# Two-block transformer on one core: expert 31's rows joined to the tokens by diagonal products on TensorE, and one root for two norms

## The reference, cut to what matters

```
y = ypad.reshape(-1, D)[dest] * weights[order][:, None]
f = zeros.at[tok].add(y)              # two weighted expert rows for each token
x = x + g2 * f                        # g2: a row of modulation gates
...
h = modulate(rmsnorm(x, norm_mix_g[1]), sh1, sc1)       # layer 1 begins, behind expert layer 0
...
x = rmsnorm(x, final_g)                                 # behind expert layer 1
h = rms_norm(x, attn_pre_norm)                          # layer 2 begins
```

## Time and profile before

| What | Value |
| --- | --- |
| median of three runs | 2109.87 us |
| profiled execution, its own time | 2111.29 us |
| its span, first to last instruction | 2109.4 us |
| PE busy, matmuls | 1954.9 us, 93% of the span |
| DVE, ACT, POOL busy | 653.6, 370.9, 321.7 us |
| moved by DMA | 586.23 MB, 278 GB/s in the mean |
| mean granted TensorE clock | 0.992 of 2.4 GHz |

### The profile page before, as it was taken

One profiled execution on the slowest core, in us unless ns is written; L12 is line 12 of the kernel. 1 busy time (PEld: TensorE's weight loads), 2 busy tenths in 40 slices (PEclk: granted clock), 3 DMA queues, 4 the chain that ended last, 5 costly groups with the idle time before them and its releaser, 6 DMA issues.

```text
span 2109.4 us, 34164 instructions
## 1 busy us (share of the span) xinstructions
PE 1954.9 (93%) x14831; PEld 1224.5 (58%) x14831; DVE 653.6 (31%) x1520; ACT 370.9 (18%) x821; POOL 321.7 (15%) x264
## 2 busy tenths in 40 slices
PE   5999999999999979999999888888789989989998
PEld 4566475555555546546565444444367677675884
DVE  1235273322222234114331111111146031037752
ACT  3133230000000002113320000000021130042131
POOL 0125402000001000114310000000120060040120
PEclk9999999999999999999999999999999999999999
DMA  9585199999999988317299999999984323427221
GB/s 362 124 274 205 56 357 381 427 426 427 426 427 422 426 347 261 118 52 281 95 381 426 427 427 426 427 426 426 407 293 151 131 81 135 145 81 200 81 92 60
DMA packets 133744, 586.23 MB, mean 278 GB/s; under 512 B 19162, under 2 KB 34474, under 8 KB 108880
## 3 DMA queue, kind: packets, MB, share of 16 engines
q1 hardware_dynamic: 117024, 558.65, 67.4%
q10 hardware_dynamic: 10448, 18.88, 3.0%
q0 software_dynamic: 6112, 6.39, 0.9%
HBM read 572.23 MB, written 25.29 MB: 283 GB/s over the span
## 4 chain that ended last, share of the span: by engine, by line
PE 69%; DMA 20%; DVE 3%; issue 3%; ACT 2%; POOL 2%; SPq 1%; DVEq 0%; POOLq 0%; ACTq 0%
DMA RG<-in_moe_w 19%; PE banks L1574 13%; PE banks L2627 8%; PE banks L1599 6%; PE banks L1550 4%; PE banks L2219 4%; PE banks L2629 4%; PE banks L1119 4%; PE banks L683 3%; PE banks L2221 3%; PE banks L2828 3%; PE banks L3039 2%; POOL AR L931 2%; PE banks L341 2%; PE banks L824 2%
## 5 line engine op out<-in xcount | busy, mean ns | idle before, releaser
L1574 PE MATMUL banks<-RG,HT 128*64 128x256 f32 x3616 | 427.8, 390 | 36.6 <-DMA RG<-in_moe_w 33.6
L1574 PEld LDWEIGHTS banks<-RG,HT 128*64 128x64 f32 x3616 | 252.6, 135 | 223.3 <-DMA RG<-in_moe_w 55.5
L1844 POOL DMA_INDIRECT y_rows<-AR x64 | 63.9, 999 | 839.8 <-DVE AR L1613 812.1
L1583 DVE TENSOR_TENSOR AR<-AR,banks 128x256 f32<-128x256 f32 x64 | 38.6, 603 | 479.6 <-ACT AR L1579 428.4
L1599 PE MATMUL banks<-RG,AR 128*64 128x512 f32 x752 | 171.7, 598 | 3.8 <-DVE AR L1592 3.1
L2627 PE MATMUL banks<-HT,RG 128*128 128x256 f32 x768 | 168.0, 380 | 0.8 <-ACT HT L550 0.8
L2627 PEld LDWEIGHTS banks<-HT,RG 128*128 128x128 f32 x768 | 145.4, 190 | 22.8 <-issue 2.4
L1579 ACT ACTIVATE AR<-banks 128x256 f32<-128x256 f32 x64 | 24.5, 383 | 744.6 <-PE banks L1574 744.6
L1550 PE MATMUL banks<-AR 128*128 128x256 bf16 (+1 forms) x1152 | 149.4, 277 | 2.0 <-DVE AR L1538 1.5
L1550 PEld LDWEIGHTS banks<-AR 128*128 128x128 bf16 x1152 | 108.3, 99 | 33.8 <-issue 18.3
L1599 PEld LDWEIGHTS banks<-RG,AR 128*64 128x64 f32 x752 | 50.0, 136 | 94.4 <-issue 83.4
(11 more groups left out here) (490 smaller groups left out, 2392.6 us busy)
## 6 DMA issues: line engine op xcount, KB each, us to landing
RG<-in_moe_w SPq DMA_DIRECT2D x160, 2048.0 KB
AR<-in_moe_w SPq DMA_DIRECT2D x32, 2048.0 KB, 21.5
RG<-in_ada_w SPq DMA_DIRECT2D x24, 2048.0 KB
RG<-in_attn_w_in SPq DMA_DIRECT2D x20, 2048.0 KB
RG<-in_odd_w_in SPq DMA_DIRECT2D x6, 2048.0 KB
RG<-in_ssm_w_in SPq DMA_DIRECT2D x4, 2048.0 KB
AR<-y_rows SPq DMA_DIRECT2D x12, 512.0 KB, 6.1
RG<-in_even_w_in SPq DMA_DIRECT2D x2, 2048.0 KB
```

The source lines that it names most:

```text
L1574: m = pe.matmul(p[64 * h:64 * h + 64, 256 * i:256 * i + 256], x[:, k, :], w[:, h, k], start=k == 0, stop=k == 7, skip_group_check=True)
L1844: g.indirect_dma_start(y, off, E.Y[b], None, bounds_check=2047, oob_is_err=False).then_inc(*event)
```

## The change

In both expert layers the join of tiles 0 and 1 moves from DVE to PE. PE starts the sum in banks 0 to 3 with a product of the identity and the residual rows (pe_own_rows, between expert 31's turns and its down products), adds the one-hot products of expert 31, whose rows DVE now scales by their weight in the slot (dve_y_last), and adds the products of the z rows with diagonals of the weights (pe_joined_rows). The weight for each slot comes from three bf16 parts of WL and eight (four) small products in the table of group 7; the parts and the diagonals are made at expert 12. pe_overflow now stands ahead of the joining products. Squares are read from PSUM, half a row at a time; the first norm's squares are added from two sums. Behind layer 0 the idle products are 10 and not 36. Behind layer 1 AG is not scaled: the turns are products with a diagonal of the norms' common factor. That factor comes from one root of mean(AF^2) + 1e-6 * (mean(x^2) + 1e-6); the root for the output's norm follows behind the turns. The idle products are 30 and don't wait, and of each tile's two banks DVE copies the second to HT. Tiles 2 and 3 of layer 0 stay as they are, but for the weight.

```diff
+                self.W3, self.WS = new(nt, 3, dt=BF), new(1)
...
+            if g == 7:
+                for h in range(2):
+                    for t in range(E.nt):
+                        m = pe.matmul(bank[64 * h:64 * h + 64, 16:19], E.one_hot(7, t)[:, 192:256], E.W3[:, t],
+                                      start=t == 0, stop=t == E.nt - 1, skip_group_check=True)
...
+            if g == 7:
+                vstep(v, v.tensor_reduce(E.WS, bank[:, 16:19], AX, ADD))
...
+        def dve_y_last(v, E, b, event):
+            v.scalar_tensor_tensor(out=E.YL, in0=PS[6 + b], scalar=E.WS, in1=(GATE0[0], GATE1)[E.l], op0=MUL,
+                                   op1=MUL).then_inc(*event)
...
+        def act_joined_squares(act, l, t, junk, name):
+
+            act.wait_ge(*at("last_out", l, t))
+            act.activation(junk[:, 512:1024], PS[2 * t + 1], ACT.Square,
+                           accum_out=ST[:, 8 + t:9 + t]).then_inc(*ev("squares_half", "joined", l, t))
+            act.wait_ge(*at("joined_half", l, t))
+            act.activation(junk[:, 0:512], PS[2 * t], ACT.Square, accum_out=ST[:, t:t + 1]).then_inc(*ev("squares", name))
+
+        def dve_joined_halves(v, l, t, first, second):
+
+            v.wait_ge(*at("last_out", l, t))
+            first(PS[2 * t]).then_inc(*ev("joined_half", l, t))
+            v.wait_ge(*at("squares_half", "joined", l, t))
+            return second(PS[2 * t + 1])
+
+        def pe_own_rows(pe):
+            for t in range(2):
+                for h in range(2):
+                    pe.matmul(PS[2 * t + h], IDN[:], XS[:, t, 512 * h:512 * h + 512], start=True, stop=False,
+                              skip_group_check=True)
+
+        def pe_joined_rows(pe, E, t):
             if t == 0:
                 pe.wait_ge(*at("last_hot", E.l))
                 pe.wait_ge(*at("y_out", E.l, 31))
             for h in range(2):
                 r = slice(64 * h, 64 * h + 64)
-                m = pe.matmul(PS[last_banks(E, t)[h]], E.LP[r, 128 * t:128 * t + 128], E.YL[r, :], start=True, stop=True)
+                pe.matmul(PS[2 * t + h], E.LP[r, 128 * t:128 * t + 128], E.YL[r, :], start=False, stop=False,
+                          skip_group_check=True)
+            pe.wait_ge(*at(f"z_load{t}", E.l, 1))
+            for c in range(2):
+                for h in range(2):
+                    m = pe.matmul(PS[2 * t + h], E.DW[t][c], E.Z[t][c][:, 512 * h:512 * h + 512], start=False, stop=c == 1,
+                                  skip_group_check=True)
+            m.then_inc(*ev("last_out", E.l, t))
...
-                ins = v.scalar_tensor_tensor(out=x, in0=PS[last_banks(E, t)[h]], scalar=E.WL[:, t:t + 1], in1=x, op0=MUL,
-                                             op1=ADD)
+                ins = v.tensor_tensor(x, PS[last_banks(t)[h]], x, ADD)
...
+                if e == 31:
+                    pe_own_rows(pe)
                 pe.wait_ge(*at("h_out", l, e))
                 pe.wait_ge(*landed(("w2", l, e)))
...
+        def dve_last_weights(v, E):
+
+            vstep(v, v.tensor_copy(E.W3[:, :, 0], E.WL))
+            for i in range(2):
+                vstep(v, v.tensor_tensor(E.WL, E.WL, E.W3[:, :, i], SUB))
+                vstep(v, v.tensor_copy(E.W3[:, :, i + 1], E.WL))
+            for t in range(2):
+                for c in range(2):
+                    ins = v.tensor_scalar(E.DW[t][c], IDN[:], E.WT[:, t, c:c + 1], None, MUL)
+            vstep(v, ins)
...
+                if e == 12:
+                    dve_last_weights(v, E)
...
         def pe_odd_begin(pe):
             pe_odd_cols(pe)
-            pe_keep(pe, 36, 3)
+            for t in range(2):
+                pe_joined_rows(pe, E0, t)
+            pe_keep(pe, 10, 5)
             for t in range(2):
                 pe_odd_turn(pe, t)
...
             for i in range(2):
-                v.wait_ge(*at("last_added", 0, i))
-                dve_odd_join(v, i, ev("joined_rows", i))
-            for i in range(2):
+                x = XS[:, i, :]
+                dve_joined_halves(v, 0, i, lambda p: v.tensor_copy(x[:, 0:512], p),
+                                  lambda p: v.tensor_copy(x[:, 512:1024], p)).then_inc(*ev("joined_rows", i))
+                v.wait_ge(*at("squares", ("mix1", i)))
+                vstep(v, v.tensor_tensor(ST[:, i:i + 1], ST[:, i:i + 1], ST[:, 8 + i:9 + i], ADD))
                 dve_rstd(v, ("mix1", i), D, at_=i)
                 dve_diagonal(v, i)
             for i in range(2):
...
             pe_experts(pe, E1, nothing)
+            pe_overflow(pe, E1)
             for t in range(2):
-                pe_last(pe, E1, t)
-            pe_overflow(pe, E1)
+                pe_joined_rows(pe, E1, t)
...
         def act_final(act):
             act.activation(ST[:, 63:64], IDN[:, 0:1], ACT.Sqrt)
             for t in range(2):
-                act.wait_ge(*at("combined", t))
-                act.activation(ar((0, 2)[t] * KK, D), XS[:, t, :], ACT.Square,
-                               accum_out=ST[:, t:t + 1]).then_inc(*ev("squares", ("final", t)))
+                act_joined_squares(act, 1, t, ar((0, 2)[t] * KK, D), ("final", t))
                 act.wait_ge(*at("gained", t))
                 act.activation(E1.Z[t][1], AF[t], ACT.Square,
                                accum_out=ST[:, 2 + t:3 + t]).then_inc(*ev("squares", ("dil", t)))
+            act_root(act, ("dil", 1), n=2, at_=2)
             act_root(act, ("final", 1), n=2, at_=0)
-            act_root(act, ("dil", 1), n=2, at_=2)
-            act.wait_ge(*at("gained", 2))
-            act.wait_ge(*at("dil_scale"))
-            act.activation(W1[1], AG, ACT.Copy, scale=ST[:, 53:54]).then_inc(*ev("dil_scaled"))
             for t in range(2):
-                act_turn(act, "dil", t)
+                act_turn_half(act, "dil", t, 0)
 
         def dve_final(v):
             v.wait_ge(*at("final_loads", 1))
             for t in range(2):
-                v.wait_ge(*at("last_added", 1, t))
-                v.wait_ge(*at(f"z_load{t}", 1, 1))
-                dve_join(v, E1, t, ev("combined", t))
-                v.wait_ge(*at("combined", t))
-                v.tensor_tensor(AF[t], XS[:, t, :], FG, MUL).then_inc(*ev("gained", t))
-            v.wait_ge(*at("gained", 1))
-            v.tensor_tensor(AG, AF[1], PG1, MUL).then_inc(*ev("gained", 2))
-            first, second, s2, w = ST[:, 16:18], ST[:, 18:20], ST[:, 2:4], ST[:, 52:54]
-            dve_rstd(v, ("final", 1), D, n=2)
-            vstep(v, v.tensor_tensor(w, first, first, MUL))
+                dve_joined_halves(v, 1, t, lambda p: v.tensor_tensor(AF[t][:, 0:512], p, FG[:, 0:512], MUL),
+                                  lambda p: v.tensor_tensor(AF[t][:, 512:1024], p, FG[:, 512:1024], MUL)).then_inc(
+                    *ev("gained", t))
+                v.wait_ge(*at("gained", t))
+                v.tensor_tensor(AG[t], AF[t], PG1, MUL)
+            s1, s2, w, a = ST[:, 0:2], ST[:, 2:4], ST[:, 18:20], ST[:, 52:54]
+            v.wait_ge(*at("squares", ("final", 1)))
+            vstep(v, v.tensor_tensor(s1, s1, ST[:, 8:10], ADD))
+            dve_mean(v, ("final", 1), s1, D)
+            v.wait_ge(*at("mean", ("final", 1)))
+            vstep(v, v.tensor_scalar(a, s1, 1e-6, None, MUL))
             v.wait_ge(*at("squares", ("dil", 1)))
-            vstep(v, v.tensor_tensor(s2, s2, w, MUL))
-            dve_rstd(v, ("dil", 1), D, n=2, at_=2, summed=True)
-            v.tensor_tensor(w, first, second, MUL).then_inc(*ev("dil_scale"))
-            v.wait_ge(*at("dil_scale"))
-            v.scalar_tensor_tensor(out=W1[0], in0=AF[0], scalar=w[:, 0:1], in1=PG1, op0=MUL, op1=MUL).then_inc(
-                *ev("normed", "dil", 0))
+            v.scalar_tensor_tensor(out=s2, in0=s2, scalar=1.0 / D, in1=a, op0=MUL, op1=ADD).then_inc(*ev("mean", ("dil", 1)))
+            dve_rstd_pair(v, ("dil", 1), 2, 2)
+            for t in range(2):
+                v.tensor_scalar(DG2[t], IDN[:], w[:, t:t + 1], None, MUL).then_inc(*ev("diagonal", "dil", t))
+            for t in range(2):
+                v.wait_ge(*at("turned", "dil", t, 1))
+                v.tensor_copy(HT[:, 4:8, 128 * t:128 * t + 128],
+                              PS[5 + 2 * t].rearrange("p (k t) -> p k t", k=4)).then_inc(*ev("turned_dve", "dil", t, 1))
+            dve_rstd_pair(v, ("final", 1), 0, 2)
             for t in range(2):
                 v.tensor_scalar(XS[:, t, :], AF[t], ST[:, 16 + t:17 + t], None, MUL).then_inc(*ev("finished", t))
 
         def pe_final(pe):
-            pe.wait_ge(*at("gained", 0))
-            pe_keep(pe, 34, 0)
+            pe_keep(pe, 30, 7)
             for t in range(2):
-                pe_turn(pe, "dil", t, W1[t], (("normed", "dil", 0), ("dil_scaled",))[t], None)
+                pe.wait_ge(*at("diagonal", "dil", t))
+                for b in range(2):
+                    for k in range(4):
+                        m = pe.matmul(PS[4 + 2 * t + b][:, 128 * k:128 * k + 128],
```

(53 more changed lines are left out.)

22 lines of the change are left out of this document (9 added, 13 removed).

## The result

The changed kernel took 2120.63 us (median of 5 runs, 2119.0 to 2121.85) against 2109.87 for the kernel before (5 runs beside it): ratio 1.0052, 95% interval 1.0041 to 1.0063. That is slower by 10.8 us, beyond the 0.2% that a measurement can tell, and above the range forecast. The profiled execution took 2119.6 us, its span is 2117.8 (2109.4 before): 8.4 us more. The other 2.4 us of the 10.8 are those by which the two profiled executions lie off their kernels' medians. The shares of the chain hardly changed.

A forecast was written before the change was run, and what follows sets the result against it. The prediction took the PE queue, and chains on which PE waits, as the bound. Its terms, -1.8 + 0.2 + 3.3 = +1.7 us on 2109.9, gave 2111.6 us, with a range of 2107 to 2117.

The forecast's parts named there:

- part 2: Branch over the overflow experts, ahead of joining products: PE back at 779.0 and 1542.9; 0.6 us lost in second layer.
- PE works without gaps behind the stretches: Behind both layers' stretches from down products to projection, PE has no gaps, so a shift there shifts the end.
- Part 1: Four own-row products between expert 31's turns and down products, both layers: 3.43 us, down products 2.9 us later.
- rival (a): Branch exposed, reached only after the down products; PE 5.4 us later in second layer, half clock 2.2; 2122.8, chance 0.16.
- Part 3: Joining on PE in both layers: 4.3 us per tile, 8.6 for both; DVE's joins and last additions removed.
- Part 4: First layer behind the join: DVE back only at 784.9, projection at 796.7 against 798.5, so -1.8 us.
- Part 5: Second layer behind the join: idle products end 1.7 us after diagonals; projection 1563.0 against 1559.6, +3.3 us.
- Part 6: Expert loops: eight small products added to group 7's table, +0.2 us in first layer; transfers hide the second layer's four.
- The sum: Whole kernel: -1.8 + 0.2 + 3.3 = +1.7 us on the median, giving 2111.6 us.

The follow-up runs named there:

- the second layer alone: Join on PE and the one root in the second layer only, first layer as in the kernel before: 2116.36 us, ratio 1.0046 against the kernel before.
- the one with 128 more: Changed kernel plus 32 idle products (128 PE instructions) in experts 20 to 27 of the second layer: 2118.91 us, ratio 1.0038 against the kernel before.
- own rows spread: Changed kernel, own rows spread over PE's waits, 18 idle products for 30: 2110.06 us; with the second layer as before the change: 2109.49 us.
- own rows behind: Changed kernel with the four own-row products behind expert 31's down products in both layers: 2115.01 us, ratio 1.0035 against the kernel before.

## Why the prediction was wrong

The step that failed most is the price of the branch in the second layer (part 2): 0.6 us of idle PE and no clock drop stood there, and the runs showed 2.5 us and 1.7 us of half clock. The second is the sentence that PE works without gaps behind the stretches: the rest grew by 2.7 us. The parts one by one:

- **Part 1, own rows:** right. They take 3.44 us, and the down products start 2.9 us later in both layers.
- **Part 2, the branch:** the mechanism was right (reached while the queue still works), its size too small. The load of the count was reached with the first down product (772.7 and 1536.1), 2.9 us behind the end of the wait, in the later half of the 1.5 to 3.5 us. In the first layer PE was back 13.7 us behind the up products, as forecast, since the branch was the short one there. The second layer's branch took 6.1 us, as assumed, but 1542.9 is what the early end of the range gives with it. The late end, 1544.7, is what came: 1543.11 with up products that start 1.6 us earlier. PE lost 2.5 us ahead of the joined rows where 0.6 stood: **+1.9**.
- **The clock behind it:** priced in rival (a) alone, at 2.2 us. It came with the smaller stall too and cost 1.7 in the second layer: **+1.7**. The forecast counted a stall of 0.6 us and no drop.
- **Part 3, joined rows:** 4.29 us a tile was 4.69 (1.06 for the one-hot products, 3.63 for the full ones). **+0.8** in the second layer, +1.0 in the first, where the second tile took 4.93.
- **Part 4, first layer:** -1.8 forecast, -1.0 measured; and 0.9 of that 1.0 was DVE's slower return in one execution of the kernel before. What is left against the other execution is 0.2. DVE came back from its own jump at 778.0, not at 784.9; that didn't set the end, as PE's idle products ended at 790.17, behind the first diagonal (786.4).
- **Part 5, second layer:** the idle products ended last, as forecast, by 1.8 us (1.7 forecast). The turns with their copy took 4.4 for 4.7, the idle products 6.7 for 6.9. The stretch: +3.3 forecast, +7.3 measured; 1.9 + 1.7 + 0.8 - 0.3 - 0.2 = 3.9 of the 4.0 missed.
- **Part 6:** the table of group 7 took 0.64 us where it took 0.51 (+0.1 for +0.2).
- **"Behind them PE works without gaps, so a shift there shifts the end":** wrong. The rest of the kernel grew by 2.7 us (3.5 by the means of two profiles each). There are gaps, and they move when the code does: one stall and the half clock behind it cost 3.4 and 3.7 us in the two profiles.
- **The sum:** profile against profile 8.4 where 1.7 stood. The 6.7 us missed are 4.0 in the second layer, 0.8 in the first, 2.7 in the rest, 0.8 between the stretches, and -1.6 up to expert 31 (-1.4 where +0.2 stood); the last two are within the spread of executions. Rival (a) came nearest in number (2122.8), by another mix: its sequencer reached the branch when the down products had run, 5.4 us late; it was 1.9 late, and the first layer lost nothing to it.

Shown by runs: the branch's exposure with its half clock (4.1 us with its code left out, the same with it moved behind), the own rows' place, the idle products' excess, that the stall behind the projection moves with the code, and that at its new place, with the half clock behind it, it makes up what the rest grew by, within 0.7 us. Not settled: why the first layer's branch took 3.5 to 4.0 us in nine of the fourteen profiles and 6.1 to 6.6 in the five where own rows stood behind the down products or the branch behind the joined rows; what decides the place of the later stall; and why single half-clock stretches differ between two executions of one kernel.

## What to carry to other kernels

The jump over the overflow block took PE's sequencer 3.5 to 6.6 us at every place where it was tried; put such a jump where more work than that is already queued, and when work is moved into or out of the queue ahead of it, work out again how much cover is left. Spread new PE work over the waits that its queue has anyway, and cut idle products when what they bridge gets shorter. When a change adds or removes instructions, expect other stretches to move (here by up to 3.7 us), and look at them before explaining a 0.2% difference.

## What the runs showed of the hardware that was not expected

- The time of PE's branch over the same block: 3522 to 4004 ns or 6055 to 6622 ns in the first layer, 6045 to 6325 in the second.
- The same jump on DVE, in the first layer: 5.7, 4.9, 5.0 and 4.9 us from the compare to the next instruction in the four profiles with the old form of that layer, 0.6 us in all ten with the new form. No run shows why.
- Straight code stalls too: 3.77 and 3.78 us in two executions of one kernel between the same two small products, 1.47 and 1.89 us in two of the other.
- The granted clock behind a PE idle in these stretches. In the second layer it was 0.50 behind 3.35 us in the changed kernel, and behind 3.25 to 3.47 us in its second execution, the second layer alone and the one with 128 more; 1.00 behind 1.64 us (own rows spread) and 0.65 us (own rows behind). In the first layer it was 0.50 behind 2.16 and 2.02 us (the two with own rows spread), 1.00 behind 1.31 us (changed). In the kernel before, an idle of 2.89 us ahead of the same transposes was followed by 0.53 in one execution, and one of 3.02 us by 1.00 in the other.
